# Attention on one core: probabilities turned in 32x32 blocks by VectorE, values on four row groups of TensorE, queries turned beside the input products

## Chip, cores and metric

The kernel runs on one core of a Trainium2 chip. The metric is device time in microseconds (us), the median over executions. The engines are TensorE (PE in the profile, with its weight loads as PEld), VectorE (DVE), ScalarE (ACT), GpSimd (POOL) and SyncE (SP), which issues most of the DMAs.

## The reference, cut to what matters

One layer of a hybrid backbone on 512 latent and 128 context tokens of width 1024, in float32. One input product gives the queries, keys and values of two attentions and two gates. After the attentions come the branch products, the output product, a mixture of 16 experts, and the final norm.

```python
def gqa_block(qb, k, v):
    s = jnp.einsum('bqhgd,bshd->bhgqs', qb, k).astype(jnp.float32) * (HEAD_DIM ** -0.5)
    p = jax.nn.softmax(s, axis=-1).astype(v.dtype)
    return jnp.einsum('bhgqs,bshd->bqhgd', p, v)

def diff_block(qb, k, v, lam):
    s = jnp.einsum('bqhmd,bshmd->bhmqs', qb, k).astype(jnp.float32) * (HEAD_DIM ** -0.5)
    p = jax.nn.softmax(s, axis=-1)
    a = p[:, :, 0] - lam[None, :, None, None] * p[:, :, 1]
    return jnp.einsum('bhqs,bshe->bqhe', a.astype(v.dtype), v)
```

There are 8 plain heads of 64 (two heads of keys and values) and 4 differential heads with two maps of 64 and values of 128. A latent query sees 256 cached and 512 latent keys; a context query sees the 128 context keys alone.

## The kernel before, in words

**Before the attention.** PE runs the input products one after another: qa, qb, kv, kb, vb, each of 640 tokens in five tiles. A weight is split into a high part (ACT, L532) and a remainder (DVE, L537), and three passes of 512 columns (L772 to L774) give a product. Each product goes through its weights in four halves; in a half, each token tile takes six matmuls. Groups of four 128x128 turns of keys (`turn_keys`, L918) stand between halves of kb and between tiles of vb; ACT copies what they give (`key_copy`, L1324). ACT makes the four splits that vb's last part and the product behind it need ahead of vb's tiles (`lead(4, ...)`); DVE makes their remainders, and then the rotary work on its own keys, in four tiles (`by_position`, L466 to L469). SP copies each query map twice side by side within SBUF (`q_first`, `q_second`, `q_third`, L635 to L648).

**The attention.** 16 maps stand in 8 pairs (`PAIRS`): the first four are pairs of plain heads (`PLAIN`), the last four are the two maps of a differential head. A pair has five query tiles (`NT`): four latent ones with 768 keys and one of the context with 128. A pair and a tile (`PUS`) are two units (`UNITS`), one for each map. The loop runs over these 40, and in each step the engines do the work of several units:

- PE: `scores` (L982 to L999) into two pairs of PSUM banks, 64 rows of weights each, two row groups side by side (L994); `turn_queries` (L972 to L980), five 128x128 turns for a map, some steps ahead; `turn_probs` (L1001 to L1015), 12 turns for a plain latent tile and 6 for a differential one, in pieces of four, `LAG` = 2 steps behind; `values` (L1017 to L1039) in three blocks for a pair, two tiles of queries (256 columns) at a time, into bank 7.
- DVE: `row_max` (L1801, L1803) straight from PSUM; `inverse_sums` (L1808); `normalise`: two multiplications for plain heads (L1817, L1818), for differential ones a multiplication with lambda (L1821) and the combining instruction a x 1/sum - b (L1824); and the third piece of turned probabilities of a plain tile from PSUM to `p_t` (L1834).
- ACT: `exponent` with the sum of a row (L1416), the copies of turned queries (L1394) and of turned probabilities (L1404) from PSUM, and `output_block` (L1425).
- POOL: nothing.

The orders are written out by hand, each engine its own list; `PIECES` numbers what passes through the turn banks 4 to 6.

**The end.** Behind the last exponent PE runs the first steps of the product ga0 (`first_gates`, L1041 to L1049) between the last turns and values. SP then brings three rows of the split input back from HBM (`ht`, `SPILLED` = 3, L649 to L652), which the product needs at its fourth half.

Of the kernel before, what the change touches and what calls it, by code (L numbers as in the profile page):

```python
# [146 lines left out]
LAG = 2  # L147
PREP = {m: max(-1, NT * (m // 2) - 4 + m % 2) for m in range(MAPS)}


QUERY_SLOTS = {PREP[m] for m in range(2, MAPS)}
PUS = [(p, t) for p in range(PAIRS) for t in range(NT)]
PLAIN = PAIRS - HB
BLOCKS = [(p, b) for p in range(PAIRS) for b in range(3)]
BLK_OF = {i: BLOCKS.index((p, min(t // 2, 2))) for i, (p, t) in enumerate(PUS)}
BLK_END = {BLK_OF[i]: i for i in range(len(PUS))}


SLOTS = len(PUS) + LAG + 3
PIECES, Q_PIECES, P_PIECES = [], {}, {}  # L160
for _i in range(-1, SLOTS):
    for _m in range(MAPS):
        if PREP[_m] == _i:
            Q_PIECES[_m] = []
            for _part in range(2):
                Q_PIECES[_m].append(len(PIECES))
                PIECES.append(("q", _m, _part))
    if 0 <= _i - LAG < len(PUS):
        _p, _t = PUS[_i - LAG]
        P_PIECES[_i - LAG] = []  # L170
        _tiles = range((KTL if _t < NTL else 1) * (2 if _p < PLAIN else 1))
        for _o in range(0, len(_tiles), 4):
            P_PIECES[_i - LAG].append(len(PIECES))
            PIECES.append(("dve" if _o == 8 else "act", _i - LAG, _tiles[_o:_o + 4]))
# [4 lines left out]
SPILLED = 3  # L179


def pieces_before(kind, n):
    return sum(1 for p in PIECES[:n + 1] if p[0] == kind)
# [4 lines left out]
KEY_GROUPS = [("a", 0, 0), ("b", 0, 0), ("b", 0, 1), ("a", 1, 0), ("a", 2, 0), ("a", "ctx", 0), ("b", "ctx", 0),  # L188
              ("b", 1, 0), ("b", 1, 1), ("b", 2, 0), ("b", 2, 1)]
# [44 lines left out]
def build(nc, x_prompt, x_sample, cache_attn_k, cache_attn_v, cache_diff_k, cache_diff_v, c, c_ctx,  # L234
# [5 lines left out]
    with ctx:  # L240
# [78 lines left out]
        probs = [at(f"probs{n}", o, [P, KTL * P]) for n, o in enumerate((0, 69120, 72192, 3072, T0 + 20992, T0 + 24064))]  # L319
        q_t = at("q_t", 58880, [P, 4, TOK])  # L320
        q_first = at("q_first", T0, [P, NT, 2, HD])
        q_second = at("q_second", 80384, [P, NT, 2, HD])
        y_t = at("y_t", T0, [P, 8, TOK])
        p_t = at("p_t", RING + 8192, [P, 2, 2 * KTL, 2 * P])
        p_ctx = at("p_ctx", T0 + 27136, [P, 2, P])
        q_third = at("q_third", T0 + 17920, [P, NT, 2, HD])
# [70 lines left out]
        ht_dram = nc.dram_tensor("ht_dram", [P, SPILLED, TOK], F32R).ap()  # L397
        x1_dram = nc.dram_tensor("x1_dram", [TOK, D], F32).ap()
# [27 lines left out]
        s_qt = sem("s_qt")  # L426
        s_sc = sem("s_sc"); s_max = sem("s_max"); s_exp = sem("s_exp"); 
        s_nrm = sem("s_nrm"); s_c1 = sem("s_c1"); s_comb = sem("s_comb"); s_ptr = sem("s_ptr")
        s_ph = sem("s_ph"); s_pl = sem("s_pl"); s_pv = sem("s_pv"); s_oev = sem("s_oev");
# [18 lines left out]
        s_q2 = [sem("s_q2a"), sem("s_q2b")]; s_yme = sem("s_yme");   # L448
# [100 lines left out]
        def two_of(m):  # L549
            return q_second if m % 2 else q_third if m else q_first  # L550

# [6 lines left out]
        def turn_bank(n, cols):  # L558
            return bank(4 + n % 3, 0, cols)

        def prob_part(i, n):

            _, t = PUS[i]
            tiles = PIECES[n][2]
            src = turn_bank(n, len(tiles) * P).rearrange("p (b c) -> p b c", c=P)
            if t == NTL:
                return p_ctx[:, 0:len(tiles), :], src
# [709 lines left out]
        def _(act):  # L1277
# [128 lines left out]
            def exponent(s):  # L1406
                _, t = UNITS[s]
                act.wait_ge(s_max, s + 1)
                if s >= 6:
                    prob_buffer_free(act, s)  # L1410
# [1019 lines left out]
```

## Time and profile before

| | us |
|---|---|
| median of the runs | 1145.94 |
| lowest and highest of the runs | 1145.12, 1146.94 |
| the profiled execution | 1145.81 |
| its span | 1144.0 |
| PE busy in it | 1097.6 |
| DVE, ACT, POOL busy in it | 528.1, 363.2, 132.4 |

The span is the time from the first to the last instruction of the profiled execution; 1.8 us lie around it. A busy time is the time in which an engine had an instruction running. The chain that ended last is followed back from the last instruction, at each step to what released it. A timeline's row merges neighbouring instructions of a kind: start, length, engine, line, tiles, shapes and count, and in brackets the idle time before it with what ended it.

### The profile page before, as it was taken

The page shows a single profiled execution, that of the slowest core. Times are in us where ns is not written, and L with a number is a line of the kernel's source. Part 1 is how long each engine was busy: PE and PEld are TensorE (multiplying, and loading weights), DVE is VectorE, ACT ScalarE, POOL GpSimd, SP SyncE. Part 2 cuts the span into 40 slices and gives each one's busy share as a digit, 9 for nine tenths or more (in the row PEclk, how much of TensorE's full clock was granted, in tenths as well). Part 3 has the DMA queues.
Part 4 walks back from the last instruction along what each step waited for, and adds up shares of the span by engine and source line. Part 5 has one row for each costly group of instructions (what it writes and reads, how often), then busy time and mean ns, then how long its engine had stood idle before and what let it go on. Part 6 is the DMA issues. An engine that isn't in the chain of part 4 may idle for free.

```text
span 1144.0 us, 28118 instructions
## 1 busy us (share of the span) xinstructions
PE 1097.6 (96%) x12524; PEld 828.2 (72%) x12524; DVE 528.1 (46%) x961; ACT 363.2 (32%) x846; POOL 132.4 (12%) x173
## 2 busy tenths in 40 slices
PE   6999999999999999999998999999999999999993
PEld 4679875666677777777877877777777777777761
DVE  4574538879958142334976033332233223333235
ACT  4333327778753223022163221222222222211103
POOL 2332300000000000002012111111110111110021
PEclk9999999999999999999999999999999999999997
DMA  9932242111031545359987999999999999999993
GB/s 359 299 107 68 77 84 63 35 31 41 1 109 38 184 147 147 106 190 300 355 303 320 402 398 406 407 405 409 414 406 405 408 404 408 405 408 405 410 321 143
DMA packets 86747, 295.32 MB, mean 258 GB/s; under 512 B 27249, under 2 KB 28530, under 8 KB 62050
## 3 DMA queue, kind: packets, MB, share of 16 engines
q1 hardware_dynamic: 79104, 269.77, 61.5%
q0 software_dynamic: 6528, 20.10, 6.1%
q10 hardware_dynamic: 994, 3.65, 0.9%
q8 instruction: 99, 1.62, 0.6%
q14 instruction: 22, 0.18, 0.0%
HBM read 273.25 MB, written 15.00 MB: 252 GB/s over the span
## 4 chain that ended last, share of the span: by engine, by line
PE 85%; DMA 7%; issue 2%; ACT 2%; DVE 2%; SPq 1%; POOLq 0%; POOL 0%; ACTq 0%; DVEq 0%
PE ps L1207 39%; PE ps L772 10%; PE ps L774 9%; PE ps L773 9%; PE ps L994 4%; PE ps L1013 3%; PE ps L1032 2%; PE ps L1036 2%; DMA x_dram<-y_row,rows_t 2%; DMA x_dram<-xn_p 1%; DMA raw_first<-in_w_in_dram 1%; DMA x_f<-x_dram 1%; PE ps L794 1%; DMA raw<-in_w_in_dram 1%; PE ps L978 1%
## 5 line engine op out<-in xcount | busy, mean ns | idle before, releaser
L2124 DVE SCALAR_TENSOR_TENSOR y_row<-ps,gates,gate_q 32x256 f32<-32x256 f32 (+1 forms) x184 | 88.3, 480 | 238.5 <-PE ps L1207 236.0
L1564 ACT ACTIVATE h_t<-ps 128x256 f32<-128x256 f32 x48 | 15.0, 384 | 374.7 <-PE ps L1207 374.7
L772 PE MATMUL ps<-w_hi,ht 128*128 128x512 f32 (+1 forms) x320 | 124.2, 388 | 0.6 <-DVE q_n L1728 0.6
L774 PE MATMUL ps<-w_hi,ht 128*128 128x512 f32 (+1 forms) x320 | 121.8, 381 | 0.0
L773 PE MATMUL ps<-raw_lo,ht 128*128 128x512 f32 (+1 forms) x320 | 121.7, 380 | 0.0
L1207 PE MATMUL ps<-late,xe 128*32 128x256 f32 x1824 | 103.6, 379 | 0.0
L537 DVE TENSOR_TENSOR raw_lo<-raw,w_hi 128x1024 fp32r<-128x1024 f32 x48 | 58.2, 1234 | 78.9 <-ACT w_hi L532 78.2
L1207 PEld LDWEIGHTS ps<-late,xe 128*32 128x32 f32 x1824 | 77.0, 110 | 23.3
L1207 PE MATMUL ps<-raw,xe 128*32 128x256 f32 x1392 | 88.1, 379 | 0.9 <-issue 0.8
L532 ACT ACTIVATE w_hi<-raw 128x1024 fp32r<-128x1024 f32 x48 | 48.7, 1053 | 123.6 <-DMA raw<-in_w_in_dram 68.1
L2354 POOL DMA_INDIRECT xg<-x_dram,rows x48 | 46.1, 961 | 320.7 <-PE ps L1207 293.2
L1554 ACT ACTIVATE xe<-xt,mods_q 128x64 f32<-128x64 f32 x240 | 77.9, 420 | 7.5 <-DVE gates L2108 7.5
L1207 PE MATMUL ps<-raw_gate,xe 128*32 128x256 f32 x1248 | 77.7, 379 | 0.0
L1207 PEld LDWEIGHTS ps<-raw,xe 128*32 128x32 f32 x1392 | 62.1, 110 | 18.6 <-issue 2.4
L772 PEld LDWEIGHTS ps<-w_hi,ht 128*128 128x128 f32 x320 | 60.1, 188 | 18.2 <-issue 5.2
L1207 PE MATMUL ps<-late,ht 128*32 128x256 f32 x1200 | 71.9, 379 | 1.0 <-issue 1.0
L1416 ACT ACTIVATE probs<-ps,neg_max 128x768 f32<-128x768 f32 (+1 forms) x80 | 63.0, 795 | 29.5 <-DVE neg_max L1801 27.5
L1801 DVE TENSOR_REDUCE neg_max<-ps 128x1 f32<-128x768 f32 x64 | 58.3, 953 | 28.9 <-PE ps L994 28.9
L774 PEld LDWEIGHTS ps<-w_hi,ht 128*128 128x128 f32 x320 | 60.0, 188 | 12.9
L773 PEld LDWEIGHTS ps<-raw_lo,ht 128*128 128x128 f32 x320 | 60.1, 188 | 11.6
L1207 PEld LDWEIGHTS ps<-raw_gate,xe 128*32 128x32 f32 x1248 | 55.9, 110 | 14.8
L1207 PEld LDWEIGHTS ps<-late,ht 128*32 128x32 f32 x1200 | 51.8, 110 | 16.8 <-issue 1.5
(315 smaller groups left out, 1831.0 us busy)
## 6 DMA issues: line engine op xcount, KB each, us to landing
late<-in_w_exp_down_dram SPq DMA_DIRECT2D x25, 1024.0 KB, 20.4
late<-in_w_exp_up_dram SPq DMA_DIRECT2D x21, 1024.0 KB, 28.8
late<-in_w_exp_gate_dram SPq DMA_DIRECT2D x17, 1024.0 KB, 24.7
raw<-in_w_in_dram SPq DMA_DIRECT2D x16, 1024.0 KB, 5.5
raw<-in_w_exp_gate_dram SPq DMA_DIRECT2D x16, 1024.0 KB
raw_gate<-in_w_exp_up_dram SPq DMA_DIRECT2D x14, 1024.0 KB
raw<-in_w_exp_up_dram SPq DMA_DIRECT2D x13, 1024.0 KB
raw_gate<-in_w_exp_down_dram SPq DMA_DIRECT2D x13, 1024.0 KB
```

The costliest lines, as they stand in the source:

```text
L532: act.activation(w_hi[:, n % NHL, :], raw_half(raw, h), ACT.Copy).then_inc(s_hi, 1)
L537: dve.tensor_tensor(raw_half(raw_lo, h), raw_half(raw, h), w_hi[:, n % NHL, :].bitcast(F32), ALU.subtract)\
L772: pe.matmul(b, stat_hi(k, tt), hi[:, kk, :], start=first, stop=False)
L773: pe.matmul(b, stat_hi(k, tt), lo[:, kk, :], start=False, stop=False)
L774: mm = pe.matmul(b, stat_lo(k, tt), hi[:, kk, :], start=False, stop=last)
L994: mm = pe.matmul(bank(b + f, 0, KEY_PAIRS * P), q_t[rows, m % 4, tt], keys_t[rows, x, :], start=True, stop=True)
L1207: mm = pe.matmul(out[32 * q:32 * q + 32, :], x[:, k, :], columns_of(w, q), start=(k == 0), stop=(k == KD - 1))
L1416: act.activation(dst, src, ACT.Exp, bias=neg_max[:, s % 8:s % 8 + 1], accum_out=row_sum[:, s % 8:s % 8 + 1]).then_inc(s_exp, 1)
L1554: a = act.activation(xe[:, n % 2, sets, k, :], xt[:, sets, k, :], ACT.Identity, scale=mods_q[:, k, v:v + 1], bias=mods_q[:, k, 2 + v:3 + v])
L1801: dve.tensor_reduce(nm, src[:, :, 0:384], AX.XY, ALU.max, negate=True).then_inc(s_max, 1)
L2124: return dve.scalar_tensor_tensor(y_row[n % 2][32 * v:32 * v + count, 256 * q:256 * q + 256], bank(b, o, o + 256, src), gates[src, n % EG, ...
L2354: pool.indirect_dma_start(xg[:, n % 2, v, :], None, x2_quarters[:, :], bass.IndirectOffsetOnAxis(ap=rows[:, v, n:n + 1], axis=0))\
```

## The change

The probabilities are no longer turned by PE. POOL normalises (two multiplications for a plain tile, one with lambda for a differential one); DVE combines the two maps of a differential tile and turns probabilities from SBUF to SBUF in 32x32 blocks with one `transpose` of 128x768. So a block of 32 keys comes to lie on 32 partitions, and the values need each block of 32 rows of v on all four quarters of the partitions: v goes to HBM (`v_dram`) and comes back repeated four times (`v_rep`, four DMAs for each load). Values are matmuls on four row groups of 32 rows into banks 4 to 7, 24 key blocks (8 in each of three parts) and 4 for the context tile; the parts of a pair stand in the first three steps of the next pair, and the last pair's behind `first_gates`. The queries are turned once, in ten groups of four within kb and vb; ACT copies and sends them to HBM (`q_dram`), and SP loads each map twice into `q_t`. ACT's splits move from ahead of vb to its halves. Ten rows of `ht` are spilled instead of three, needed at the second half.

```diff
+VALUE_PARTS = 3
+KB, KBL = KEYS // 32, (PAST + LAT) // 32
-SPILLED = 3
+SPILLED = 10
-KB_KEYS = {1: ("a", 1, 0), 2: ("a", 2, 0), 3: ("a", "ctx", 0)}
-VB_KEYS = {(2, 1): ("b", "ctx", 0), (2, 4): ("b", 1, 0), (3, 0): ("b", 1, 1), (3, 1): ("b", 2, 0), (3, 2): ("b", 2, 1)}
+KB_KEYS = {0: [("q", 0, 0), ("q", 1, 0)], 1: [("a", 1, 0), ("q", 2, 0)], 2: [("a", 2, 0), ("q", 3, 0)],
+           3: [("q", 0, 1), ("a", "ctx", 0)]}
+VB_KEYS = {(0, 0): ("q", 4, 0), (0, 3): ("q", 5, 0), (1, 1): ("q", 6, 0), (1, 3): ("q", 7, 0), (2, 0): ("q", 4, 1),
+           (2, 1): ("b", "ctx", 0), (2, 4): ("b", 1, 0), (3, 0): ("b", 1, 1), (3, 1): ("b", 2, 0), (3, 2): ("b", 2, 1)}
...
+                    def load_query(m):
+                        if m >= 4:
+                            sp.wait_ge(s_sc, U_LAST[m - 4] + 1)
+                        if m % 2 == 0 and m:
+                            sp.wait_ge(s_qt, 32 * m)
+                        for f in range(2):
+                            sp.dma_start(q_t[HD * f:HD * f + HD, m % 4, :], q_dram[HEAD[m]]).then_inc(s_qt, 16)
...
+                        for a in range(4):
+                            sp.dma_start(v_rep[values_of(p)][32 * a:32 * a + 32, :, :],
+                                         v_dram[:, h, :].rearrange("(b c) n -> c b n", c=32)).then_inc(s_vrep, 16)
...
-                    sp.wait_ge(s_ptr, len(PIECES))
+                    sp.wait_ge(s_pv, PAIRS - 1)
                     sp.dma_start(ht[:, 0:SPILLED, :].bitcast(F32), ht_dram.bitcast(F32)).then_inc(s_refill, 16)
...
+            def values(p, part):
+                w, pt = v_rep[values_of(p)], p_t[(p + 1) % 2]
+                heads = 2 if p < PLAIN else 1
...
+                n = KBL // VALUE_PARTS
+                for b in range(part * n, part * n + n):
+                    for a in range(4):
+                        for v in range(heads):
+                            rows, cols = slice(32 * a, 32 * a + 32), slice(P // heads * v, P // heads * (v + 1))
+                            mm = pe.matmul(bank(4 + a, 0, P, cols), w[rows, b, cols], pt[rows, v, :, b, :], start=(b == 0),
+                                           stop=(b == KBL - 1))
...
+            for i in range(len(PUS)):
...
                 if i + 1 < len(PUS):
                     scores(2 * i + 2)
                     scores(2 * i + 3)
+                p, t = PUS[i]
+                if p and t < VALUE_PARTS:
+                    values(p - 1, t)
+            pe.wait_ge(s_exp, len(UNITS))
+            pe.wait_ge(s_lo, SPLIT_OF[gemm_half(5, 0)] + 1)
+            first_gates(0, range(NTL))
+            for part in range(VALUE_PARTS):
+                values(PAIRS - 1, part)
...
+                if kind == "q":
+                    g4 = Q_GROUPS.index(group)
+                    act.activation(q_stage[:, g4 % 4, :], bank(6 + n % 2), ACT.Copy).then_inc(s_kev, 1)
+                    act.wait_ge(s_kev, n + 1)
+                    if g4:
+                        act.wait_ge(s_qst, 16 * g4)
...
+                        act.dma_start(dst, q_stage[:, g4 % 4, :]).then_inc(s_qst, 16)
...
-            lead(4, end_b + 2)
-            for hh in (2, 3):
+            for hh in range(4):
+                if hh < 3:
+                    split_hi(act, gemm_half(4, hh) + 2)
+                if hh == 2:
+                    split_hi(act, gemm_half(4, 3) + 2)
                 for t in range(NT):
                     if (hh, t) in VB_KEYS:
                         key_copy(VB_KEYS[hh, t])
...
+            for i in range(len(PUS)):
+                if i + 1 < len(PUS):
+                    row_max(2 * i + 2)
+                inverse_sums(i)
+                if i:
+                    turn_probs(2 * i - 2)
+                if i + 1 < len(PUS):
+                    row_max(2 * i + 3)
+                if i:
+                    turn_probs(2 * i - 1)
...
+                    if v == 0:
+                        dve.wait_ge(s_second, i + 1)
+                        dve.scalar_tensor_tensor(a, a, row_inv[:, o:o + 1], b, ALU.mult, ALU.subtract).then_inc(s_comb, 1)
+                        return
...
+                dve.transpose(dst.rearrange("p b r -> p (b r)"), prob_row(s)[:, 0:n]).then_inc(s_ptr, 1)
...
+            for i, (p, t) in enumerate(PUS):
...
+                pool.wait_ge(s_inv, i + 1)
+                if p < PLAIN:
+                    pool.tensor_scalar(a, a, row_inv[:, o:o + 1], one, ALU.mult, ALU.mult).then_inc(s_nrm, 1)
+                    pool.tensor_scalar(b, b, row_inv[:, o + 1:o + 2], one, ALU.mult, ALU.mult).then_inc(s_second, 1)
+                else:
+                    pool.tensor_scalar(b, b, row_inv[:, o + 1:o + 2], lam[:, g:g + 1], ALU.mult, ALU.mult)\
+                        .then_inc(s_second, 1)
```

## Rows read from the trace of the kernel before

**Rows 1.** The page: share of the chain that ended last, by engine.
```profile
PE 85%; DMA 7%; issue 2%; ACT 2%; DVE 2%; SPq 1%; POOLq 0%; POOL 0%; ACTq 0%; DVEq 0%
```

**Rows 2.** Windows: us, busy us and instructions of each engine, clock, DMA share, GB/s.
```profile
203.60:223.60 20.00, 20.00 (x149) 12.80 (x150) 15.71 (x31) 14.52 (x37) 0.00 (x0) 1.00 0.16 34
265.40:282.37 16.97, 16.97 (x100) 11.87 (x99) 15.43 (x26) 13.35 (x37) 0.00 (x0) 1.00 0.19 40
```

**Rows 3.** Timeline (start us, us): end of vb, first scores, first maxima.
```profile
168.90 0.71 PE L978 MATMUL ps<-tab,q_first 128*128 128x128 f32 x5
...
170.53 1.56 PE L994 MATMUL ps<-keys_t,q_t 64*128 64x384 f32 x8
...
171.57 1.82 DVE L1801 TENSOR_REDUCE neg_max<-ps 128x1 f32<-128x768 f32 x2 [16.67 <-PE ps L994]
```

**Rows 4.** Timeline of DVE: maxima of pairs 0, 1, 4 and 7; last output copy.
```profile
185.65 0.48 DVE L1803 TENSOR_REDUCE neg_max<-ps 128x1 f32<-128x128 f32 x2
...
205.67 0.48 DVE L1803 TENSOR_REDUCE neg_max<-ps 128x1 f32<-128x128 f32 x2
...
264.15 0.49 DVE L1803 TENSOR_REDUCE neg_max<-ps 128x1 f32<-128x128 f32 x2
...
266.39 1.81 DVE L1801 TENSOR_REDUCE neg_max<-ps 128x1 f32<-128x768 f32 x2
...
314.59 0.48 DVE L1803 TENSOR_REDUCE neg_max<-ps 128x1 f32<-128x128 f32 x2
...
325.85 0.28 ACT L1425 ACTIVATE y_t<-ps 128x128 f32<-128x128 f32 x1 [0.64 <-PE ps L1036]
```

**Rows 5.** Timeline of product vb on PE and DVE.
```profile
140.57 4.63 DVE L537 TENSOR_TENSOR raw_lo<-raw,w_hi 128x1024 fp32r<-128x1024 f32 x4 [3.91 <-ACT w_hi L532]
...
154.21 0.69 DVE L469 TENSOR_TENSOR k_n<-k_n,rope_d 128x512 f32<-128x512 f32 x1
...
158.54 0.39 PE L774 MATMUL ps<-w_hi,ht 128*128 128x512 f32 x1
158.77 0.60 PE L918 MATMUL ps<-tab,k_n 128*128 128x128 f32 x4
159.12 0.48 PE L772 MATMUL ps<-w_hi,ht 128*128 128x512 f32 x1
```

**Rows 6.** Groups by line and form, 168.9 to 330 us: DVE and ACT.
```profile
L1801 DVE TENSOR_REDUCE neg_max<-ps 128x1 f32<-128x768 f32 x64 | 58.3, 953 | 28.9 <-PE ps L994 28.9
...
L1824 DVE SCALAR_TENSOR_TENSOR probs<-probs,row_inv,probs 128x768 f32<-128x768 f32 x16 | 16.3, 1019 | 0.6
...
L1817 DVE TENSOR_SCALAR probs<-probs,row_inv 128x768 f32<-128x768 f32 x16 | 9.9, 621 | 0.6
...
L1808 DVE RECIPROCAL row_inv<-row_sum 128x2 f32<-128x2 f32 x40 | 6.2, 155 | 0.0
...
L1416 ACT ACTIVATE probs<-ps,neg_max 128x768 f32<-128x768 f32 x64 | 57.1, 898 | 27.5 <-DVE neg_max L1801 27.5
```

**Rows 7.** Timeline of PE: two scores; a router step with four column groups.
```profile
207.21 1.56 PE L994 MATMUL ps<-keys_t,q_t 64*128 64x384 f32 x8
...
582.24 0.64 PE L1129 MATMUL ps<-x_t,router_s 128*32 128x128 f32 x16 [0.25 <-ACT x_t L1510]
```

**Rows 8.** POOL's copies (L2263: min/median/max ns); timeline of POOL and DVE.
```profile
L2263 POOL COPY k_cache<-k_raw x2: 780/1240/1700, 48.8 to 49.5; 128x640 f32<-128x640 f32 x2
...
112.55 1.66 POOL L466 TENSOR_TENSOR rope_p<-k_n,tab 128x64 f32<-128x64 f32 x2
...
120.59 0.69 POOL L466 TENSOR_TENSOR rope_p<-k_n,tab 128x64 f32<-128x64 f32 x2
...
115.36 0.83 DVE L469 TENSOR_TENSOR q_n<-q_n,rope_d 128x512 f32<-128x512 f32 x1
```

**Rows 9.** Windows around the one fall of PE's clock behind the start.
```profile
47.00:50.70 3.70, 0.95 (x6) 0.42 (x4) 2.54 (x3) 3.70 (x6) 1.92 (x2) 0.92 1.05 385
50.70:52.50 1.80, 1.80 (x4) 1.48 (x5) 1.76 (x3) 1.57 (x4) 0.52 (x1) 0.50 1.06 369
```

More of the change, by code:

```diff
@@ L160 @@
[L160 to L174, printed above, removed]
+VALUE_PARTS = 3
@@ new lines, in _ @@
+                    sp.wait_ge(s_vah, NT)
+                    sp.wait_ge(s_vac, 16)
+                    store_values(va_n, 0)
+                    sp.wait_ge(s_qst, 16 * len(Q_GROUPS))
+                    for m in range(4):
+                        load_query(m)
+                    sp.wait_ge(s_vst, 64)
+                    sp.wait_ge(s_kout, 48)
+                    sp.wait_ge(s_kev, 3)
+                    load_values(0)
+                    sp.wait_ge(s_free_a, 3 * NT)
+                    sp.wait_ge(s_vc, 16)
@@ L909, in turn_keys @@
                     pe.wait_ge(s_kev, n - 1)
-                if u == "ctx":
+                if kind == "q" and g:
+                    sources = [q_n[:, NTL, 2 * j:2 * j + 2, :] for j in range(u, u + 4)]
+                elif kind == "q":
+                    sources = [q_n[:, t, 2 * u:2 * u + 2, :] for t in range(NTL)]
+                elif u == "ctx":
                     maps = range(KVA) if kind == "a" else range(KVA, KMAPS)
@@ new lines, in values @@
+            def values(p, part):
+                w, pt = v_rep[values_of(p)], p_t[(p + 1) % 2]
+                heads = 2 if p < PLAIN else 1
+                if part == 0:
+                    pe.wait_ge(s_vrep, values_loaded(p))
+                    pe.wait_ge(s_ptr, TURNED[NT * p + NTL - 1])
+                    if p:
+                        pe.wait_ge(s_oev, p)
+                n = KBL // VALUE_PARTS
[5 more added lines that the diff above has]
+                                           stop=(b == KBL - 1))
+                if part == VALUE_PARTS - 1:
+                    pe.wait_ge(s_ptr, TURNED[NT * p + NTL])
+                    for b in range(KBL, KB):
+                        for a in range(4):
+                            for v in range(heads):
+                                rows, cols = slice(32 * a, 32 * a + 32), slice(P // heads * v, P // heads * (v + 1))
+                                mm = pe.matmul(bank(4 + a, P, P + 32, cols), w[rows, b, cols], p_ctx[rows, (p + 1) % 2, v, b - KBL, :],
+                                               start=(b == KBL), stop=(b == KB - 1))
@@ L1368, in _ @@
                 split_hi(act, gemm_half(3, hh) + 2)
-                if hh in KB_KEYS and hh < 3:
-                    key_copy(KB_KEYS[hh])
+                for group in KB_KEYS[hh][:1] if hh == 3 else KB_KEYS[hh]:
+                    key_copy(group)
             for t in range(NT):
@@ L1836, in _ @@
+                if p >= 2:
+                    dve.wait_ge(s_pv, p - 1)
+                if t < NTL:
+                    dst, n = p_t[(p + 1) % 2][:, v, t, :, :], KTL * P
+                else:
+                    dst, n = p_ctx[:, (p + 1) % 2, v, :, :], P
+                dve.transpose(dst.rearrange("p b r -> p (b r)"), prob_row(s)[:, 0:n]).then_inc(s_ptr, 1)
+            dve.wait_ge(s_spill, 16)
             row_max(0)
             row_max(1)
-            for i in range(SLOTS):
-                if 1 <= i <= len(PUS):
-                    inverse_sums(i - 1)
-                    normalise(i - 1)
-                if 0 <= i - LAG < len(PUS) and i not in QUERY_SLOTS:
-                    probs_turned(i - LAG)
+            for i in range(len(PUS)):
```

341 lines of the change are left out of this document (112 added, 229 removed).

## The prediction

> **What bounds the kernel now.** I read the page first: TensorE (PE) holds 85% of the chain that ended last [rows 1], so a change counts where it moves PE's order of work or what PE waits for. Next the windows: in a plain pair of heads PE is busy for 20.00 of 20.00 us with VectorE (DVE) at 15.71, in a differential pair 16.97 of 16.97 with DVE at 15.43 [rows 2]. So the attention is bound by PE, with DVE close behind; POOL does nothing there. The timeline gives the frame: the last input product ends at about 168.9, queries are turned until 170.5, the first maximum starts at 171.57 [rows 3]. The maxima of the context tile, the last tile of each pair, give the pairs: 14.1 us from the first maximum to the first of them, 20.0 from there to the next (185.65 to 205.67), 58.5 for the next three, 50.4 for the last three (264.15 to 314.59) [rows 3, 4]. The last output copy ends at 326.1 [rows 4].
>
> **The change part by part.** *Removed from PE in the attention:* 300 turns of probabilities and 80 of queries; in its place, per pair, 24 key blocks of values on four row groups. *Added before the attention:* ten groups of four query turns in the products kb and vb. A group of four already stands there. Product matmuls follow each other by 0.23 (158.54, then the group at 158.77); the next one stands at 159.12 and lasts 0.48 instead of 0.39, so it could start 0.08 later still [rows 5]: 0.43 us each, so 10 x 0.43 = **+4.3 us**, since PE is busy throughout these products. The group q01 makes ScalarE's (ACT) copies of the kb bank later, and vb's first query group waits for it: I put a copy's 0.6 us there, **+0.6**.
>
> *A step moved in a queue:* the four splits of weight halves that ACT did at the start of vb stand now one by one behind query copies, the last two behind the copy of q70 at vb's half 1, tile 3. DVE makes its four remainders (4.63 us from 140.57, waiting for the splits, L532) behind them, and behind the remainders, in order, the rotary work on its own keys: four tiles to 154.9, 2.43 us each [rows 5]. After: a tile step of vb is 1.40 us (six matmuls of 0.233). The group at 158.77 is that of half 2, tile 4; q70's place is six steps and one group before it, 149.9, and 0.6 and nine new groups move it to 154.4. Its copy ends at 155.3; two splits and the last remainder, each about a remainder's 1.16, end at 158.8; three key tiles, which the group at (2,4) needs, at 158.8 + 3 x 2.43 = 166.1. PE gets there at 158.77 + 0.6 + 10 x 0.43 = 163.7. So PE waits 2.3 to 2.4: **+2.3**. vb ends 7.2 later, at 176.1. The scores then start at once, as no query is turned between; that takes back 1.6 us of 168.90 to 170.53 [rows 3]. **Start of attention: +5.6 us.**
>
> *The loop.* DVE now has, for a plain latent tile, two maxima of 0.953, one reciprocal of 0.155 and two transposes of 128x768 [rows 6]. No DVE transpose stands in this trace. Bounds: 0.62, the tensor_scalar of the same size (L1817), and 1.02, the combining instruction with two inputs (L1824) [rows 6]. I take 0.95, that of the maximum: it is the row with one input of full width and no sign of a doubled rate. Instructions that follow each other overlap by 0.08 (two maxima take 1.82, not 1.91 [rows 3]); so 1.91 + 0.155 + 1.90 - 5 x 0.08 = 3.56 us. A differential tile: 1.91 + 0.155 + 1.02 + 0.95 - 0.4 = 3.63.
>
> Does anything else take longer? A score buffer's ring is maximum 0.95, exponent 0.90 [rows 6], score 0.9, and three handovers with the reading of the sum: 3.2 to 3.3. PE: two scores are 1.5 us (1.56 with the drain) [rows 7], and a third of the values is eight blocks. In the row of L1129, four column groups of 128 columns run side by side: 16 matmuls in 0.64 us [rows 7], that is four rounds of 0.109 and 0.2 to fill and drain. So eight rounds are 0.87 + 0.2 = 1.07, if four row groups do the same. With it the ring is 3.4, still under DVE. POOL: a copy of 128x640 took 0.78 at best [rows 8], so 768 take 0.94, two of them 1.9: hidden under 3.56. ACT loses its copies from PSUM and has two exponents, 2.2. The context tile has little work but the same chain of handovers; between its maxima and the next latent ones lie 2.2 us now (264.15 to 266.39 [rows 4]); I take 2.4. So a plain pair is 4 x 3.56 + 2.4 = 16.7, a differential one 4 x 3.63 + 2.4 = 16.9.
>
> Against [rows 4]: first pair 4 x 3.56 = 14.2 against 14.1, **0**; three plain steps 3 x (16.7 - 20.0) = **-9.9**; the step into the differential pairs 17.0 against 18.5 (the rest of the 58.5), **-1.5**; three differential steps 50.7 against 50.4, **+0.3**. Beside POOL, DVE's instructions with two inputs took 0.83 where they take 0.69 alone (L469 [rows 5, 8]); the combine has two inputs as well, so 16 x 0.1 us: **+1.5**. The tail: from the last context maxima to the end of the last output copy 11.5 us (314.59 to 326.1 [rows 4]); after, the last exponents 1.1, twelve matmuls of first gates 2.8, three parts of values 1.07 x 3 + 0.4, two output copies 1.0, handovers 0.5: 9.0, **-2.5**. **Loop and tail: -12.1 us.**
>
> *At nothing:* loads of the queries, of the repeated values and the refill of ten rows rather than three (3.3 MB) run on DMA queues that have little else here; the refill is issued about 24 us before its use (8 in the last pair, 9 in the tail, 7 in a product half). If that cover were gone it would cost up to its own length, 8.5 us at the 385 GB/s of [rows 9]. The stages behind follow PE's order as before and move with it.
>
> Sum: 5.6 - 12.1 = -6.5 us. The profiled execution took 1145.81 (span 1144.0), 0.13 under the median of the runs, so 1139.3, and I write **1139.5**.
>
> **A rule weighed.** POOL was slowed by DVE: its two rope products took 1.66 us beside DVE's two-input work and 0.69 after it had ended [rows 8]; DVE lost only 0.1 to 0.14. In the loop POOL's first multiplication is released by the reciprocal, and the combine is DVE's next instruction, so DVE is there first. The Trainium skill ("SBUF — State Buffer", section "SBUF: two separate sides") says that DVE with two SBUF inputs and a reading GpSimd exclude each other for a whole instruction, whoever starts first. The trace agrees in kind for POOL (2.4 times as long) but not for DVE's share. By that rule with POOL first, each combine would wait out a POOL instruction; that is a rival below.
>
> **The rivals.**
> *Faster than forecast* (12%): transposes at 0.62, and keys not late. Tiles fall to the ring, 3.56 to 3.3 and 3.63 to 3.5, 16 x 0.26 + 16 x 0.13 = -6.2, and -2.3: 1131.
> *Slower than before* (15%): the row groups do not run four at a time. The trace shows two row groups together (L994: eight matmuls of 384 columns in 1.56 us, four rounds of 0.32 and the ends) but no four [rows 7]. It decides from where scores, values and the ring pass DVE's 3.56. Two at a time: a part takes 1.94, the ring with it 3.85; 21 parts x 0.3, seven context blocks x 0.4 and 3.0 in the tail: +12, 1151.5 (10%). One at a time: 3.6 a part, PE 1.5 + 3.6 + switches = 5.3, 21 x 1.75 + 10 = +47: 1186 (5%).
> *POOL becomes the bound* (13%): the copy took 1.70 at worst [rows 8], for 768 elements 2.0; two and their start are 4.1 for 3.56, 16 x 0.5 = +8, 1147.5; for a combine that waits out each POOL instruction, 16 x 0.94 = +15, 1154 at the worst; mostly less: 1140 to 1151.
> *The gain is lost behind* (5%): refill or weights hold the next products: 1144 to 1147.
> *DVE at half rate, or the clock* (9%). PE is idle now half of a tile without values. The clock fell here once: PE was busy 0.95 of 3.70 us, then ran at 0.50 of full speed, the 1.2 GHz level [rows 9]. Gaps in the new loop would be near 1 us, which speaks against. At that level scores and values take twice as long, about like two row groups at a time or somewhat worse: 1151 to 1160. Transposes of 1.75: 16 x 1.5 + 16 x 0.7: +35.
>
> **How the numbers follow.** The forecast has 46%; its own range is 1135 to 1143 (transposes 0.85 to 1.02, start +3 to +6). A measurement here tells 0.2%, 2.3 us. Faster by more: 46 + 12 + 2 of POOL's = 60%. Within: 8 of POOL's + 5 = 13%. Slower: 15 + 3 + 9 = 27%. The range takes in the faster rival, POOL and two row groups at a time: 1131 to 1152; outside lie one row group at a time, most of the half rate and clock, and the ends.
>
> **What would show it.** First score near 176.1; a wait of PE on DVE's keys in vb of some 2 us; transposes of 0.95; context maxima 16.7 apart in plain pairs and 17 in the others; DVE busy nearly all the time in the loop; values parts of about 1.07 with no wait on POOL. Parts of 1.9, a clock under 1.00, POOL instructions over 1.7, or a later time behind the attention than at its end would make the prediction wrong.

## The result and the profile after

The changed kernel takes 1167.61 us (median; 1167.01 to 1169.15) against 1146.09: a ratio of 1.019, 95% interval 1.0172 to 1.0208. It is 21.5 us slower where 6.5 less were forecast, and outside the range. The profiled execution took 1167.01 (span 1165.2, 21.2 over the span of before); the sums below are in that execution.

The page's share of the chain that ended last, by engine, of the changed kernel:

```profile
PE 78%; DVE 8%; DMA 6%; issue 4%; ACT 2%; POOL 1%; ACTq 0%; SPq 0%; POOLq 0%; DVEq 0%
```

PE had 85% and DVE 2% [rows 1]. The attention has become a chain that goes back and forth between DVE and PE. Where the 21.2 us came in is told by a few marks, read from the timelines of both kernels. The context maxima of before are [rows 4], and for pair 3 this row of the same timeline; the first mean of a head starts at 329.84 before and at 348.81 now.

```profile
245.66 0.48 DVE L1803 TENSOR_REDUCE neg_max<-ps 128x1 f32<-128x128 f32 x2
```

| from | to | before | after | difference |
|---|---|---|---|---|
| start | first score | 170.5 | 177.4 | +6.8 |
| first score | context maxima of pair 0 | 15.1 | 14.4 | -0.7 |
| pair 0 | pair 1 | 20.0 | 25.9 | +5.9 |
| pair 1 | pair 3 | 40.0 | 38.0 | -2.0 |
| pair 3 | pair 4 | 18.5 | 18.5 | 0.0 |
| pair 4 | pair 7 | 50.4 | 55.9 | +5.5 |
| pair 7 | mean of the first head | 15.25 | 18.75 | +3.5 |
| mean of the first head | end | 814.2 | 816.4 | +2.2 |

The timeline of DVE in the changed kernel, maxima of the context tiles of pairs 0, 1, 3, 4 and 7 (start us, length, then what ended the idle time):

```profile
191.75 0.25 DVE L1746 TENSOR_REDUCE neg_max<-ps 128x1 f32<-128x128 f32 x1
...
217.66 0.29 DVE L1746 TENSOR_REDUCE neg_max<-ps 128x1 f32<-128x128 f32 x1 [2.39 <-PE ps L983]
...
255.64 0.29 DVE L1746 TENSOR_REDUCE neg_max<-ps 128x1 f32<-128x128 f32 x1 [0.58 <-PE ps L983]
...
274.12 0.29 DVE L1746 TENSOR_REDUCE neg_max<-ps 128x1 f32<-128x128 f32 x1 [1.36 <-PE ps L983]
...
330.06 0.29 DVE L1746 TENSOR_REDUCE neg_max<-ps 128x1 f32<-128x128 f32 x1 [0.79 <-PE ps L983]
```

These answer to [rows 4]: 25.9 us stand between the first two, 18.5 between pair 3 and pair 4. The brackets at the context maxima of pairs 1, 3, 4 and 7 say that DVE waits there for a score of PE (L983). Forecast were 16.7 and 16.9 for a pair.

**The start.** Timeline of PE in the products kb and vb and at the first score (answers to [rows 3, 5]):

```profile
142.07 0.63 PE L924 MATMUL ps<-tab,q_n 128*128 128x128 f32 x4 [0.67 <-ACT q_stage L1274]
...
167.07 0.66 PE L924 MATMUL ps<-tab,k_n 128*128 128x128 f32 x4 [2.62 <-DVEq L1734]
...
177.35 0.92 PE L979 MATMUL ps<-keys_t,q_t 64*128 64x384 f32 x4
```

A query group waits 0.67 for ACT's copy, the key group of half 2, tile 4 of vb waits 2.62 for DVE's work on its own keys, and the first score stands at 177.35.

**The instructions.** Groups by line and form of the changed kernel, 160 to 355 us (busy us, mean ns, idle before):

```profile
L1776 DVE STREAM_TRANSPOSE p_t<-probs 128x768 f32<-128x768 f32 x48 | 46.1, 961 | 0.0
...
L1000 PE MATMUL ps<-p_t,v_rep 32*64 32x128 f32 x1536 | 28.1, 288 | 4.6 <-issue 4.6
...
L2251 POOL TENSOR_SCALAR probs<-probs,row_inv,lam 128x768 f32<-128x768 f32 x16 | 24.0, 1501 | 41.2 <-DVE row_inv L1751 41.2
...
L1761 DVE SCALAR_TENSOR_TENSOR probs<-probs,row_inv,probs 128x768 f32<-128x768 f32 x16 | 16.0, 997 | 0.0
...
L2248 POOL TENSOR_SCALAR probs<-probs,row_inv,tab 128x768 f32<-128x768 f32 x16 | 15.7, 981 | 42.4 <-DVE row_inv L1751 42.4
```

The transposes take 961 ns each and POOL's plain multiplication 981: both as forecast (0.95, 0.94). The row of the values tells the first thing that was not: 1536 matmuls for four pairs. The code writes 8 blocks x 4 row groups x 2 heads x 3 parts x 4 pairs = 768. Each float32 matmul of the code stands as two in the trace.

**A clean pair.** Timeline of PE and DVE in the step from pair 3 to pair 4, where the clock was 1.00 throughout and nothing stalled for long:

```profile
262.49 2.10 PE L1000 MATMUL ps<-p_t,v_rep 32*64 32x128 f32 x128
...
264.52 1.56 PE L979 MATMUL ps<-keys_t,q_t 64*128 64x384 f32 x8
265.48 0.96 DVE L1744 TENSOR_REDUCE neg_max<-ps 128x1 f32<-128x768 f32 x1 [1.70 <-PE ps L979]
...
270.22 2.10 PE L1000 MATMUL ps<-p_t,v_rep 32*64 32x128 f32 x128
...
272.81 0.85 PE L1008 MATMUL ps<-p_ctx,v_rep 32*64 32x32 f32 x64 [0.50 <-issue]
...
274.12 0.29 DVE L1746 TENSOR_REDUCE neg_max<-ps 128x1 f32<-128x128 f32 x1 [1.36 <-PE ps L983]
```

A part of the values takes 2.10 us. Behind the first one the next scores come late, and DVE waits 1.70; behind the third and the blocks of the context tile it waits 1.36. In the other tiles of the pair a maximum follows that of the tile before by 3.5 to 3.6 us with hardly a wait, as forecast (3.56 and 3.63).

**The stall in pair 1.** Windows of the changed kernel (us, busy us of PE, PEld, DVE, ACT, POOL with instructions, clock, DMA share, GB/s), and under them the timeline of PE:

```profile
199.00:203.00 4.00, 4.00 (x170) 3.02 (x170) 2.26 (x6) 1.83 (x5) 1.92 (x2) 1.00 1.25 181
203.00:207.60 4.60, 0.66 (x41) 0.42 (x25) 2.62 (x4) 1.97 (x4) 1.94 (x2) 0.87 0.60 137
207.60:212.00 4.40, 4.39 (x77) 3.19 (x79) 0.36 (x1) 0.00 (x0) 0.00 (x0) 0.50 0.01 4
```

```profile
202.52 1.14 PE L1000 MATMUL ps<-p_t,v_rep 32*64 32x128 f32 x57
207.61 2.41 PE L1000 MATMUL ps<-p_t,v_rep 32*64 32x128 f32 x71 [3.95 <-issue]
```

PE stops after 57 of 128 matmuls of a part, waits 3.95 us for nothing that the profile's semaphores show ("issue"), and goes on at half clock. The DMA view of the same stretch shows what it could wait for, first 199 to 205 us, then 205 to 208 (queue, packets, MB, time of the packets as a share of 16 engines):

```profile
q1 hardware_dynamic: 1599, 1.21, 118.5%
q14 instruction: 1, 0.01, 0.5%
```

```profile
q1 hardware_dynamic: 71, 0.13, 17.2%
q8 instruction: 1, 0.02, 2.6%
```

Until 205 the load of the first differential values, with loads of queries behind it, fills all engines (118.5%). The packet of the instruction queue q8 comes at 205.0, when these loads run out, and 2.6 us later PE goes on. That q8 brings PE's instructions is told by its packets in the whole execution, first of the changed kernel, then of the run below with half of the values' blocks:

```profile
q8 instruction: 114, 1.87, 0.6%
```

```profile
q8 instruction: 105, 1.72, 0.6%
```

PE has 14560 matmuls and as many weight loads in the first and 13408 of each in the second, 2304 instructions fewer, and there are 9 packets fewer: 256 instructions and 16 KB a packet. (q14 has 21 packets in both.) A part of plain heads is 128 weight loads and 128 matmuls, so one packet. How a load of data holds such a packet up is not told by these views.

**The clock.** Windows of two differential steps of the same work:

```profile
292.50:312.05 19.55, 16.69 (x260) 10.59 (x260) 15.67 (x26) 9.55 (x23) 7.15 (x5) 0.83 0.75 129
312.05:330.06 18.01, 14.14 (x260) 9.37 (x260) 15.55 (x25) 9.55 (x23) 7.15 (x5) 1.00 0.65 104
```

The granted clock fell to half, the 1.2 GHz level, four times between 189 and 302 us for 6.8 us each, and once in the tail for 3.4; in the kernel before it never fell in the attention (only ahead of it, [rows 9], and in both kernels over the last 15 to 18 us). DVE, ACT and POOL are busy as long in both rows; the step with a fall is 1.5 us longer, 19.55 against 18.01.

**The tail.** Timeline of PE behind the last exponent of the changed kernel:

```profile
332.09 0.51 PE L1017 MATMUL ps<-w_hi,ht 128*128 128x512 f32 x1 [2.06 <-ACT probs L1367]
...
336.63 4.74 PE L1000 MATMUL ps<-p_t,v_rep 32*128 32x128 f32 x159
341.53 1.26 PE L1000 MATMUL ps<-p_t,v_rep 32*128 32x128 f32 x33 [0.16 <-issue]
...
344.55 0.47 PE L1017 MATMUL ps<-w_hi,ht 128*128 128x512 f32 x1 [0.95 <-ACT y_t L1378]
```

PE idles 2.06 us for the last exponent, then runs the first gates in 4.5 us (332.09 to 336.63) with the clock falling, then the three parts of values from 336.63 to 343.6: 7.0 us where 3.6 were forecast.

### The profile page after: what moved, and what is told of

It reads as the page before. It is cut to its first block, busy times and chain, and to the rows that moved or that the text cites. A ratio compares the mean times of both kernels' runs of the same rounds, so it can differ in the third digit from the quotient of the medians.

```text
span 1165.2 us, 32004 instructions
## 1 busy us (share of the span) xinstructions
PE 1082.0 (93%) x14560; PEld 864.5 (74%) x14560; DVE 527.0 (45%) x945; ACT 334.0 (29%) x744; POOL 194.7 (17%) x233
## 4 chain that ended last, share of the span: by engine, by line
PE 78%; DVE 8%; DMA 6%; issue 4%; ACT 2%; POOL 1%; ACTq 0%; SPq 0%; POOLq 0%; DVEq 0%
PE ps L1160 38%; PE ps L770 9%; PE ps L772 9%; PE ps L771 9%; PE ps L1000 3%; PE ps L979 2%; DVE neg_max L1744 2%; DMA x_dram<-y_row,rows_t 2%; DVE p_t L1776 1%; DMA x_dram<-xn_p 1%; PE ps L792 1%; DMA x_f<-x_dram 1%; DMA raw<-in_w_in_dram 1%; DVE probs L1761 1%; ACT probs L1367 1%
## 5 line engine op out<-in xcount | busy, mean ns | idle before, releaser
L1160 PEld LDWEIGHTS ps<-late,xe 128*32 128x32 f32 x1824 | 87.2, 110 | 13.0
L979 PE MATMUL ps<-keys_t,q_t 64*128 64x384 f32 x256 | 62.4, 579 | 23.9 <-ACT probs L1367 23.7
L1160 PEld LDWEIGHTS ps<-raw,xe 128*32 128x32 f32 x1392 | 69.2, 110 | 13.0 <-issue 3.0
L770 PEld LDWEIGHTS ps<-w_hi,ht 128*128 128x128 f32 x320 | 60.1, 188 | 19.3 <-issue 5.2
L1160 PEld LDWEIGHTS ps<-raw_gate,xe 128*32 128x32 f32 x1248 | 62.2, 110 | 8.5
```

The source lines that it names most:

```text
L770: pe.matmul(b, stat_hi(k, tt), hi[:, kk, :], start=first, stop=False)
L979: mm = pe.matmul(bank(b + f, 0, KEY_PAIRS * P), q_t[rows, m % 4, tt], keys_t[rows, x, :], start=True, stop=True)
L1160: mm = pe.matmul(out[32 * q:32 * q + 32, :], x[:, k, :], columns_of(w, q), start=(k == 0), stop=(k == KD - 1))
```

## The experiments

Each is one edit of the changed kernel unless it says more, and only its main lines are shown; ratios are against the kernel before, with their 95% intervals. The changed kernel stands at 1.0190 (1.0172 to 1.0208).

### Half of the values' blocks

```diff
-                for b in range(part * n, part * n + n):
+                for b in range(part * n, part * n + n // 2):
...
```

> Half of the key blocks of the values are left out (four of eight in each part), so a latent tile's output lacks half of its keys. A part then has 64 matmuls of plain heads in the trace instead of 128, the eight rounds of the prediction, about 1.2 us instead of 2.1. Theory A (the part was sized at half of its length, and the part stands in the chain of scores and maxima): a pair's step falls from 18.4 to about 17, and with half the instructions to fetch the stall shrinks; 12 to 18 us less, 1150 to 1156. Rival B (the loop is bound by VectorE and the values are hidden, the loss is the stall, the clock and the start): 3 to 7 us less, 1161 to 1165.

Measured: 1149.44 us, ratio 1.0015 (1.0000 to 1.0029), 18.2 us under the changed kernel's median, a little more than expected: theory A. (Ten executions lie between 1142.9 and 1151.1.) The steps are 17.5, 17.5 and 16.2 between plain pairs, then 17.6, 17.0, 19.2 and 17.9. A part in its timeline of PE, and the window of the cleanest plain step:

```profile
238.78 1.21 PE L1000 MATMUL ps<-p_t,v_rep 32*64 32x128 f32 x64
```

```profile
228.80:244.90 16.10, 11.97 (x292) 6.71 (x292) 15.25 (x26) 9.34 (x23) 8.65 (x10) 1.00 0.16 44
```

64 matmuls in 1.21 us are the eight rounds of the prediction (1.07). A part of 128 takes 2.10, so eight rounds more cost 0.89, or 0.111 a round, close to the prediction's 0.109. The cleanest step takes 16.1, of which DVE is busy 15.25: the prediction's 16.7 with DVE as the bound. The stall of pair 1 is gone as well, with half of the values' instructions. So in the one step that ran at full clock the forecast's model of the loop holds with its own number of rounds; the number was half of the real one. The four steps behind it ran at granted clocks of 0.73 to 0.90. This run mixes what the stall gave and what the rounds gave; the next ones take the stall alone.

### The load of the differential values moved, left out, with long rows, spread

The load later:

```diff
...
-                    load_values(PLAIN)
                     for p in range(2, PAIRS):
                         load_query(2 * p)
                         load_query(2 * p + 1)
+                        if p == 3:
+                            sp.wait_ge(s_pv, 1)
+                            load_values(PLAIN)
```

> The one edit: SP brings the repeated values of the first differential pair later, behind the queries of pair 3, so in pair 2 instead of pair 1. Theory A (PE's instructions, 16 KB a packet and one packet for each part of the values, wait behind this load's packets): the 3.95 us stall in the middle of pair 1's second part goes or moves with the load to pair 2; the step of pair 1 falls from 25.9 to about 18.5. If it only moves, the time is within 3 us of 1167.6; if pair 2's parts are fetched in time, about 1160. Rival B (the stall belongs to the first run through the parts, or to the start of the values themselves): it stays in pair 1 and the time stays at 1167.6.

Measured: 1171.54 us, ratio 1.0203 (1.0175 to 1.0232), 3.9 above the changed kernel where at most 3 were expected. The long stall left pair 1 and stands in pair 2, whose step went from 19.3 to 25.3, while pair 1 went from 25.9 to 21.4. Timeline of PE in pair 2:

```profile
222.62 1.68 PE L1002 MATMUL ps<-p_t,v_rep 32*64 32x128 f32 x91
229.06 1.54 PE L1002 MATMUL ps<-p_t,v_rep 32*64 32x128 f32 x37 [4.76 <-issue]
```

After 91 of 128 matmuls PE waits 4.76 us, again as "issue". The stall goes where the load goes, which rules out rival B. The packet of q8 came here at 225.8, while the load still filled the engines (until about 228.5), so the packet does not always wait for the load's end; PE went on at 229.06. Pair 1 did not come down to 18.5 but to 21.4: a stall of 1.97 us stays at the blocks of its context tile, and the clock was down for 10.2 us at its begin.

The load left out:

```diff
...
-                    load_values(PLAIN)
...
-                        if PLAIN < p:
-                            sp.wait_ge(s_pv, p - 1)
-                            load_values(p)
...
```

> The values of the differential pairs are not loaded: all pairs multiply with the repeated values of the first load, so the differential outputs are not the reference's. The instructions of all engines but SP are the same. Theory A (PE's instruction packets and nothing else wait behind the loads of values): pair 1's stall of 3.95 us is gone and its step falls from 25.9 to about 18.5, pair 5 or 6 from 19.56 to 18; 8 to 11 us less, 1157 to 1160. Rival B (the packets are late by themselves, since a part uses 16 KB of instructions in 2 us): the stall stays, 1166 to 1168.

Measured: 1163.79 us, ratio 1.0159 (1.0135 to 1.0183). Pair 1 takes 20.6. Timeline of PE in pair 1:

```profile
201.85 2.20 PE L996 MATMUL ps<-p_t,v_rep 32*64 32x128 f32 x128
...
205.47 2.10 PE L996 MATMUL ps<-p_t,v_rep 32*64 32x128 f32 x128
...
213.88 0.34 PE L1004 MATMUL ps<-p_ctx,v_rep 32*64 32x32 f32 x15 [1.73 <-issue]
```

The parts run through in 2.20 and 2.10. A stall of 1.73 at the blocks of the context tile remains, with no transfer of data beside it; the packet of q8 came between 211.0 and 211.5, and PE went on at 213.88. So theory A is right on the long stall, and rival B has a share: packets can be late by 1 to 2 us on their own. They are so where short instructions follow each other (64 more matmuls in 0.85 us), but that this is the reason was not shown. The gain, 3.8 us, is less than the 8 to 11 expected: pairs 5 and 6 still took 19.5 and 19.6 without loads, with the clock down for 3.4 us in each.

Long rows for the load:

```diff
...
-        v_dram = nc.dram_tensor("v_dram", [KEYS, 1 + HB, P], F32).ap()
+        v_dram = nc.dram_tensor("v_dram", [1 + HB, 32, KB, P], F32).ap()
...
-                                         v_dram[:, h, :].rearrange("(b c) n -> c b n", c=32)).then_inc(s_vrep, 16)
+                                         v_dram[h]).then_inc(s_vrep, 16)
...
```

> The values are written to HBM in the order in which they are repeated, so that each of the four loads has rows of 14 KB instead of 512 bytes; the stores are 28 small ones instead of four. Theory A (the instruction packet waits behind a load that takes over 10 us because its rows are short): the load takes 4 to 6 us, pair 1's step falls from 25.9 to 19 to 21; 4 to 8 us less, 1160 to 1164. Rival B (any heavy transfer holds the packet up as long): the stall is as long, 1166 to 1168.

Measured: 1172.05 us, ratio 1.0222 (1.0205 to 1.0239): no shorter stall, as rival B has it, and 4 us above its range as well. Timeline of PE in pair 1:

```profile
203.21 1.14 PE L1003 MATMUL ps<-p_t,v_rep 32*64 32x128 f32 x57
205.71 1.35 PE L1003 MATMUL ps<-p_t,v_rep 32*64 32x128 f32 x71 [1.36 <-issue]
...
208.49 0.99 PE L1003 MATMUL ps<-p_t,v_rep 32*64 32x128 f32 x49
214.38 2.01 PE L1003 MATMUL ps<-p_t,v_rep 32*64 32x128 f32 x64 [4.90 <-issue]
```

Two stalls, 1.36 and 4.90 us. The DMA view has the engines nearly full from about 201 to 212 us: until 209 with the load of values, which takes 8 us where 4 to 6 were expected, and then with loads of queries. The long stall stands beside the queries and behind them; the packet of q8 came at 211.8. So it need not be the load of values that holds a packet up. The 28 small stores also hold SP for 15.9 us, so that this run does not weigh the length of rows by itself.

The load spread over four pairs, and ACT's splits ahead of vb:

```diff
...
+                        if p <= PLAIN + 1:
+                            sp.wait_ge(s_pv, p - 1)
+                            load_values(PLAIN, [p - 2])
...
```

> Two edits: ACT's splits ahead of vb, and the four loads of the first differential values issued one in each of four pairs, behind that pair's values, instead of all in pair 1. Theory A (a transfer holds PE's instructions up only while it runs, and 2.7 us behind the values run beside scores alone): no stall over 2 us in pair 1, its step falls from 25.9 to 19.5 to 20.5; with 0.8 to 2.7 for the splits 1158 to 1162. Rival B (the instructions are late in any case): a stall of over 3 us stays, 1165 to 1167.

Measured: 1160.41 us, ratio 1.0123 (1.0105 to 1.0141): theory A, 7.2 us under the changed kernel and the fastest version of it with all of its work. Pair 1 takes 20.2 and its longest stall is 1.59. (Its profiled execution, 1167.22, lies above its median; marks of its later pairs are not used.)

### ACT's splits ahead of vb

```diff
+            lead(4, end_b + 2)
             for hh in range(4):
-                if hh < 3:
-                    split_hi(act, gemm_half(4, hh) + 2)
-                if hh == 2:
-                    split_hi(act, gemm_half(4, 3) + 2)
```

> The one edit: ACT makes the four splits ahead of vb's tiles, as before. Theory A (VectorE's work on its own keys is late only because the remainders wait for the splits that stand behind query copies): PE's wait of 2.6 us for keys in vb goes, and the time falls by 2 to 2.7 us, to about 1165. Rival B (ACT's query copies are then late instead, and PE waits for their banks): the wait turns up at the query groups and the time stays within 1 us of 1167.6.

Measured: 1166.81 us, ratio 1.0172 (1.0155 to 1.0189). The wait for keys is gone, and the first score stands 3.2 us sooner than in the changed kernel:

```profile
174.17 1.35 PE L979 MATMUL ps<-keys_t,q_t 64*128 64x384 f32 x6
```

Theory A is right on the place. The whole kernel gained only 0.8 in the medians, within the spread: pair 1 took 27.4 instead of 25.9, with the clock down longer around its begin (10.2 us instead of 6.8), so part of the time saved ahead was lost again there.

### The clock

Extra matmuls in the first pair and behind each context tile:

```diff
-                if i < 2:
+                p, t = PUS[i]
+                if p and t == NTL:
+                    pe.wait_ge(s_oev, p)
+                    pe.matmul(bank(7, 0, KEY_PAIRS * P), ident, keys_t[:, 0, :], start=True, stop=True)
+                if not p:
...
```

> The one edit: PE gets two matmuls of 384 columns more in every tile of the first pair, and one behind each later pair's context tile, so that it idles less where no values run. Theory A (the clock falls because PE idles where the queries and probabilities were turned before): the fall near 190 us and the one in pair 5 go, the ones behind the stall in pair 1 may stay; 2 to 5 us less, 1163 to 1166. Rival B (the falls come from the stalls alone, and the first pair's maxima are bound by VectorE anyway): the clock's falls stay or cost nothing, 1167 to 1168; the added matmuls may cost up to 1 us.

Measured: 1169.49 us, ratio 1.0206 (1.0188 to 1.0224). First a window of the changed kernel around its first fall, then two of this run over the same stretch and behind it:

```profile
186.00:193.00 7.00, 3.59 (x14) 1.98 (x16) 7.00 (x12) 4.11 (x10) 4.43 (x5) 0.74 0.66 250
```

```profile
186.00:193.00 7.00, 5.47 (x21) 2.42 (x20) 6.99 (x13) 3.85 (x11) 4.44 (x6) 1.00 0.67 252
193.00:200.00 7.00, 4.69 (x65) 2.11 (x68) 6.17 (x10) 3.30 (x8) 2.57 (x4) 1.00 1.19 191
```

The fall near 190 us is gone, and the time is not less: pair 1 took 26.8, and falls came at 207, 224, 265 and 303 us. Rival B. With the loads left out as well:

> No loads of the differential values (as before, those outputs are not the reference's), and PE's extra matmuls in the first pair and behind each context tile. Against the run without the loads alone this tells what the clock's falls cost once the stall is gone. Theory A (a fall costs about as much as the values and scores in it take longer): pair 1 falls from 20.6 to about 18.5 and the falls near 195 and 215 are gone, 1160 to 1162. Rival B (the falls cost little, VectorE binds): 1163 to 1166, with the extra matmuls in the way of scores.

Measured: 1164.81 us, ratio 1.0153 (1.0129 to 1.0178), the same as without the loads alone; pair 1 took 21.6. Rival B again. Up to 352 us the clock was down for 17 us in each of the two runs with extra matmuls, in place of 31 in the changed kernel and 27 without the loads, and the times are no less: either they cost about what the clock gives back, or a fall costs little. So what the falls cost in all was not measured by these runs. The nearest rows are the two windows of differential steps in the result: 1.5 us for a fall in one step.

### Where the parts of the values stand

Four parts of six blocks (`VALUE_PARTS = 4`):

> The one edit: a pair's values are done in four parts of six key blocks instead of three of eight, in the steps of tiles 0 to 3 of the next pair. Theory A (each part of 16 rounds stands in the chain of scores and maxima, and the third part with the context blocks holds up the context tile's scores): parts of 12 rounds take 1.6 us instead of 2.1, a clean step falls from 18.0 to 18.7 to about 17.0 to 17.5, 5 to 9 us less, 1159 to 1163. Rival B (the step is bound by VectorE's 3.6 us a tile and the handovers at the context tile, wherever the parts stand): steps stay at 18.0 to 18.7, the time at 1167.6.

Measured: 1168.78 us, ratio 1.0209 (1.0177 to 1.0241); clean steps of 18.2 and 18.3. Rival B: steps don't get shorter.

Each part cut in two, a score between the halves:

```diff
...
+                for v in range(2):
+                    if i + 1 < len(PUS):
+                        scores(2 * i + 2 + v)
+                    if p and t < VALUE_PARTS:
+                        values(p - 1, t, v)
...
```

> The one edit: each part of the values is cut in two, and PE's order is score, half part, score, half part, instead of both scores and then the whole part. Theory A (a part of 2.1 us stands between two pairs of scores, so VectorE waits for the next scores): clean steps fall from 18.0 to 18.7 to 17 to 17.5, 4 to 8 us less, 1160 to 1163. Rival B (each score buffer's chain takes in the same length of values, one way or the other): steps stay within 0.3 us, 1166 to 1169.

Measured: 1170.27 us, ratio 1.0209 (1.0189 to 1.0229); clean steps of 18.2: rival B.

Parts of 4, 12 and 8 blocks, on top of the spread load and the splits:

```diff
...
-                n = KBL // VALUE_PARTS
-                for b in range(part * n, part * n + n):
+                bounds = (0, 4, 16, KBL)
+                for b in range(bounds[part], bounds[part + 1]):
...
```

> The edits of the spread loads and of the splits, and one more: the three parts of the values have 4, 12 and 8 key blocks instead of 8 each. In the changed kernel VectorE waits 1.70 us for scores behind the first part of a pair and 1.36 at the context tile, and not at all behind the second. Theory A (it is the place of a part that decides: behind the context tile VectorE has little of its own to do, two tiles later its 3.55 us cover a longer part): a clean step falls by 0.6 to 0.9 us, 4 to 6 us in all, from 1160.4 to 1154 to 1157. Rival B (the whole length of the values counts, wherever it stands): the wait turns up behind the second part, 1159 to 1162.

Measured: 1165.40 us, ratio 1.0161 (1.0144 to 1.0178). A miss for theory A: it is slower than without the uneven parts (1160.41). The wait turned up behind the second part, as rival B has it, and the long part stood still once for 1.20 us ("issue"); the clock was down longer as well (six falls of 3.4 to 13.7 us between 187 and 321 us, 51 in all, against 27 in the changed kernel). Timelines of DVE and of PE in pair 3:

```profile
245.01 0.96 DVE L1743 TENSOR_REDUCE neg_max<-ps 128x1 f32<-128x768 f32 x1 [2.76 <-PE ps L981]
```

```profile
243.47 0.65 PE L1002 MATMUL ps<-p_t,v_rep 32*64 32x128 f32 x18 [1.20 <-issue]
```

Three ways to place the same rounds gave nothing. Only fewer rounds made a clean step shorter.

### Three edits together

Splits ahead of vb, four parts and long rows:

> Three edits together: ACT's splits ahead of vb, four parts of values, and long rows for the loads of values. If their causes are apart, their gains add up: 1 to 3 for the splits, 5 to 9 for the parts, 4 to 8 for the rows; 1149 to 1157. If the clock falls wherever PE idles, whatever the cause, less of it is kept: 1157 to 1162.

Measured: 1174.22 us, ratio 1.0237 (1.0218 to 1.0256): a miss, slower than any of the three. Two of the three had no gain of their own to add, and PE waited 3.2 us for `q_t` once, whose loads SP issues behind the small stores. No version beat the kernel before.

## Why the prediction was wrong, point by point

**What bounds it, and the start: right in kind.** The wait of PE for DVE's keys was put at 2.3 and is 2.62; the group q01 at 0.6 and 0.67. The first score came 6.8 later, not 5.6. What was missed is a further 0.9: PE's wait for `q_n` of DVE ahead of a product is 1.5 in all where the page had 0.6 before.

**Transposes, POOL, DVE's 3.56 a tile: right.** 0.961, 0.981, and 3.5 to 3.6 from one tile's maximum to the next where DVE does not wait for scores. The 1.5 us for combines slowed beside POOL did not come: they take 0.997 on the average, 1.019 before [rows 6].

**The step that failed: "eight rounds are 0.87 + 0.2 = 1.07".** A part has 16 rounds and takes 2.1. The four row groups do run side by side: 128 matmuls in 2.1 us are 16 rounds of eight (four row groups with two heads each); 32 rounds of four would take 3.5 at 0.109 each. What was wrong is the count. A float32 matmul of the code stands as two matmuls in the trace, one behind the other. The rows that the prediction used show it: a router step writes 8 matmuls, and its row says x16 [rows 7]; two latent scores are four, and their row says x8. The prediction counted the rows' matmuls for the duration of a round and the code's for their number. Its rival with a part of 1.94 had the right time for a wrong reason (two row groups at a time).

With 16 rounds the prediction's own terms give +12, which is its 1151.5. Clean steps of 18.0 to 18.7 against 16.7 and 16.9 are 7 x 1.5 = 10.5 of this, and in the tail 7.0 against 3.6 us for the parts is 3.4. So DVE was busy 15.55 of 18.01 us in a step at full clock, where nearly all the time was forecast. The run with half of the blocks, 18.2 us faster, shows that this term decides, though part of its gain is the stall's.

**What no part of the prediction had: the supply of PE's instructions.** The prediction weighed the loads of values as hidden, as nothing waited for their data. None of the long waits was for their data, but PE's instructions come through the same DMA engines. The long stall costs 3.95 us and the half clock after it more; pair 1 was 25.9 against the 18.5 of the same step without it. Spread loads (with the splits) gave 7.2 us back.

**The clock: a rival at 9%, too low.** "Gaps in the new loop would be near 1 us, which speaks against" was a poor argument. In the stretch of the first fall PE was busy 3.59 of 7.00 us, and no idle time there was over 1.4 us. One fall was 1.5 us in a step. Four in the loop and one in the tail may be some 6 to 8 us, if each costs that much; this is an estimate from that row alone, and the runs with extra matmuls did not give it back. What stays open is the falls' whole price.

**The gain lost behind: a small part.** The end moved 2.2 us more than the first head's mean. The clock fell once more there, at 629.6 us; what the rest is was not followed up.

The sum, by the marks: forecast -6.5; start +1.2; first pair -0.7; the seven steps 138.3 us in place of 119.3 (three of 16.7, 17.0, three of 16.9 and 1.5), +19.0; tail +6.0; end +2.2: together +21.2. Of the steps' 19.0 some 10.5 are rounds, 7.4 pair 1 with its stall, and the rest the falls outside it, less the 1.5 that did not come. Of the tail's 6.0, 3.4 are the parts, 1.7 the first gates at a falling clock (4.5 us for 2.8), and the last exponents took 2.0 us for 1.1.

## What to carry to other kernels

Take the count and the duration of a step from the same place: multiply a row's own time per written instruction, not a round's time by the number in the code. Ask of a transfer not only who waits for its data, but what else passes through the same queues; a loop of many short matmuls needs a steady supply of instructions. Freeing an engine of work gains nothing where the chain still passes through it at each tile; here its clock fell as well.

## What the runs showed of the hardware that was not expected

PE can stand still for 3.9 to 4.9 us for want of instructions when transfers of data fill the DMA engines. Moving the load of values moved the stall, leaving it out removed it. In the stalls above, PE went on 2 to 3.5 us after a packet of q8 had come, whether the load had run out (205.0, then 207.61) or not (225.8, then 229.06).

POOL's multiplication is held up by a combine of DVE, but not by its transposes. The timeline of both in a differential tile of the changed kernel:

```profile
326.52 0.99 DVE L1761 SCALAR_TENSOR_TENSOR probs<-probs,row_inv,probs 128x768 f32<-128x768 f32 x1
...
326.70 1.67 POOL L2251 TENSOR_SCALAR probs<-probs,row_inv,lam 128x768 f32<-128x768 f32 x1 [1.91 <-DVE row_inv L1751]
```

The multiplication with lambda takes 1.67 us here and 1.50 on the average, against 0.98 in plain tiles, where DVE has transposes and maxima alone. The combine loses nothing. The Trainium skill ("SBUF — State Buffer", section "SBUF: two separate sides") says that whichever of a DVE instruction with two SBUF inputs and a GpSimd instruction that reads SBUF starts first keeps the shared ports for the whole instruction. Here the combine starts first, and the row agrees: POOL ends 0.86 after the combine, a little less than the 0.98 that it needs in plain tiles.
